# Weights and operands requested ahead of the stage that uses them, and z held feature by token

## What is computed

```python
for li in range(2):
    h = rmsnorm(x, norm_g) * (1 + scale) + shift          # same for the context hc
    if li == 0: y, yc = mixer_even(h, hc)                 # mLSTM (4 heads) and RWKV-7 (8 heads), both directions
    else:       y = column_to_raster(mixer_odd(raster_to_column(h), hc))   # HGRN (4 heads) and Hyena
    x = x + gate * y
return rmsnorm(x, final_norm_g)

# finish of the HGRN half of mixer_odd
g_y = heads_rmsnorm(from_heads(g_h), g_norm_g, HGRN_HEADS) * silu(pre['gz'])
y   = concatenate([g_y, y_y]) @ w_out
```

## Time and profile before

| | us |
|---|---|
| median of 3 runs | 2583.48 (2578.12 to 2585.52) |
| profiled execution | 2587.97 |
| its span, first to last instruction | 2585.8 |
| PE busy in the span | 2374.5 (92%) |
| DVE / ACT / POOL busy | 1434.6 / 785.2 / 229.1 |
| mean granted clock of PE | 0.96 of full speed |

### The profile page before, as it was taken

How to read it: one execution, slowest core, us unless ns; L and a number is a source line. 1 busy time by engine, 2 the same in 40 slices (tenths; PEclk the granted TensorE clock), 3 DMA queues, 4 the chain that set the end, 5 groups by cost and what they waited for, 6 DMA issues and landing times. The chain is left out here.

```text
span 2585.8 us, 52162 instructions
## 1 busy us (share of the span) xinstructions
PE 2374.5 (92%) x22964; PEld 1500.5 (58%) x22964; DVE 1434.6 (55%) x2326; ACT 785.2 (30%) x1443; POOL 229.1 (9%) x259
## 2 busy tenths in 40 slices
PE   4999999999899958998998998999898999999698
PEld 2454466666544427887884453444784676857643
DVE  5221245553367737877885454654494777778404
ACT  3111122224455623433332221101102345454301
POOL 0000000000011221111110113331100000000000
PEclk8999999999989978999999998999898999999899
DMA  6300122221065572132105422110222100000043
GB/s 259 122 11 7 33 76 66 76 72 63 30 168 163 138 180 90 61 134 101 53 28 189 143 84 66 50 56 17 82 97 81 34 26 19 25 18 10 25 172 113
DMA packets 119694, 209.23 MB, mean 81 GB/s; under 512 B 7285, under 2 KB 81141, under 8 KB 115886
## 3 DMA queue, kind: packets, MB, share of 16 engines
q1 hardware_dynamic: 105246, 152.79, 18.0%
q0 software_dynamic: 14224, 53.12, 7.2%
HBM read 155.35 MB, written 50.53 MB: 80 GB/s over the span
## 5 line engine op out<-in xcount | busy, mean ns | idle before, releaser
L786 PE MATMUL psum<-arena,m_fill_weight 128*128 128x512 f32 (+1 forms) x864 | 331.1, 528 | 6.2 <-DMA m_fill_weight<-in_l_w_in 6.2
L2707 PE MATMUL psum<-arena,g_weight 128*128 128x512 f32 (+1 forms) x512 | 224.7, 560 | 10.9 <-DMA g_weight<-in_l_w_in 10.3
L786 PEld LDWEIGHTS psum<-arena,m_fill_weight 128*128 128x128 f32 x864 | 159.5, 194 | 113.4 <-issue 98.5
L2698 PE MATMUL psum<-g_weight,arena 128*128 128x128 f32 x1152 | 157.4, 285 | 3.8 <-DMA g_weight<-in_l_w_in 3.8
L1251 PE MATMUL psum<-gp_weight,arena 128*128 128x512 f32 x320 | 147.8, 610 | 0.0
L2136 PE MATMUL psum<-fin_weight,fin_mix 128*128 128x512 f32 x320 | 143.4, 601 | 3.0 <-POOL fin_mix L2269 3.0
L2698 PEld LDWEIGHTS psum<-g_weight,arena 128*128 128x128 f32 x1152 | 141.3, 196 | 7.1 <-issue 4.4
L2707 PEld LDWEIGHTS psum<-arena,g_weight 128*128 128x128 f32 x512 | 88.6, 194 | 52.6 <-issue 35.3
L2962 DVE COPY_PREDICATED g_pairs<-g_masks,psum 128x512 f32<-128x512 uint8 x128 | 93.4, 730 | 37.2 <-PE psum L2736 36.4
L2136 PEld LDWEIGHTS psum<-fin_weight,fin_mix 128*128 128x128 f32 x320 | 59.8, 192 | 75.0 <-issue 71.5
L1251 PEld LDWEIGHTS psum<-gp_weight,arena 128*128 128x128 f32 x320 | 59.5, 194 | 72.2 <-issue 71.7
(11 more groups left out here) (443 smaller groups left out, 4309.2 us busy)
## 6 DMA issues: line engine op xcount, KB each, us to landing
arena<-scratch_operands SPq DMA_DIRECT2D x40, 512.0 KB, 3.8
scratch_operands<-arena POOLq DMA_DIRECT2D x16, 640.0 KB, 8.0
scratch_operands<-arena POOLq DMA_DIRECT2D x32, 320.0 KB, 10.7
g_weight<-in_l_w_in SPq DMA_DIRECT2D x20, 512.0 KB, 3.9
m_fill_weight<-in_l_w_in SPq DMA_DIRECT2D x18, 512.0 KB, 3.9
mod_weight<-in_l_mod_w SPq DMA_DIRECT2D x8, 1024.0 KB, 11.8
t_matrix<-in_transform SPq DMA_DIRECT2D x8, 1024.0 KB, 4.8
scratch_spill<-m_fill_shifted POOLq DMA_DIRECT2D x12, 640.0 KB, 3.2
```

Source lines behind the costliest of these rows:

```text
L786: last = nc.tensor.matmul(p.psum[:, FILL + f % BANKS, 0:width], weight[:, q % PIECES, k, :], hT[:, k, at:at + width], start=(k == 0), stop ...
L2698: last = nc.tensor.matmul(bank[:, (t - part[0]) * P:(t - part[0] + 1) * P], hT[:, kk, t * P:(t + 1) * P], w[:, kk, :], start=(kk == 0), st ...
L2707: last = nc.tensor.matmul(bank[:, 0:width], w[:, kk, :], hT[:, kk, first:first + width], start=(kk == 0), stop=(kk == KT - 1))
```

## The change

Three changes in one. (1) In the mLSTM stage `GATE_BEATS` is 20 instead of 18. (2) First layer: one buffer `shared` holds in turn the projection weights, the mLSTM fill weights, prepare's weights, the scan's values and masks, and the output weights, so that SP can load the next stage's data while a stage runs. (3) Second layer: the same with `second_shared` for Hyena's sums, HGRN's weights and gates, and the output weights; z is computed feature by token like q, and POOL multiplies it in after the turn. Semaphores of loads that cross a stage are kept for the whole program. `out_weight_of(shared)` is the first 8 x 1024 columns of the buffer. The core of the diff:

```diff
-    BANKS, PIECES, GATE_BEATS, STEP_BEATS = 2, 4, 18, 6
+    BANKS, PIECES, GATE_BEATS, STEP_BEATS = 2, M_PIECES, 20, 6
...
# stage_project, SP, after its own loads
+                if following:
+                    sp.wait_ge(products_ready, ends[len(jobs) - SLOTS])
+                    for to, of, next_loaded in following:
+                        sp.dma_start(to, of).then_inc(next_loaded, 16)
...
# stage_mlstm, SP: the first four slices are there
-                q = 0
+                q = PIECES
...
# stage_gate_and_prepare
+        v = lambda j: product[:, :] if j + 1 < R_PAIRS else kr[:, (j + 1) % 2, :]
-        opened, mixT = sb("opened", [P, 2, W]), sb("mixT", [P, 2, WT, P])
+        opened = sb("opened", [P, 2, W])
...
+        mixT = sb("mixT", [P, 3, WT, P])
...
-                sp.dma_start(kr[:, 0, :], spill[2, 0]).then_inc(kr_loaded[0], 16)
                 for i, name in enumerate(("w_up", "a_up")):
                     sp.dma_start(up[:, i, :], p.dram[name]).then_inc(sig["up_loaded"], 16)
+                sp.dma_start(kr[:, 0, :], spill[2, 0]).then_inc(kr_loaded[0], 16)
...
+                    if j + 1 < R_PAIRS:
+                        sp.wait_ge(sig["keys_ready"], 2 * j + 2)
+                    else:
+                        sp.wait_ge(sig["keys_used"], 2 * j)
+                    sp.dma_start(v(j), spill[3, j]).then_inc(sig["v_loaded" if j + 1 < R_PAIRS else "last_v_loaded"], 16)
...
+                sp.wait_ge(sig["project_ready"], UNITS)
+                sp.dma_start(scan_masks, p.dram["const_rwkv"].rearrange("p (d n) -> p d n", d=2)).then_inc(p.masks_loaded, 16)
+                sp.wait_ge(queries_stored, 48 * (ITEMS - 1))
+                sp.wait_ge(keys_stored, 48 * (ITEMS - 1))
+                window = scan_window(arena)
+                for i, c in enumerate(scan_order(0, R_CHUNKS, CTX // R_CHUNK)[0:R_EARLY]):
+                    sp.dma_start(window[:, i], operands[0, c]).then_inc(p.operands_loaded[i], 16)
+                load_values(sp, vT, spill[3], 0, R_EARLY_TOKENS, p.v_loaded)
...
# POOL, end of the block
-                pool.wait_ge(sig["bonus_stored"], 16 * R_PAIRS)
                 pool.wait_ge(queries_stored, 48 * ITEMS)
                 pool.wait_ge(keys_stored, 48 * ITEMS)
-                for i in range(2):
-                    pool.wait_ge(mix_stored[i], 16 * TILES // 2)
...
# DVE, the last gate unit ahead of the last bonus
+                    if s == END:
+                        gate(UNITS - 1)
...
# stage_rwkv_scan, SP
-                    sp.dma_start(window[:, s % SLOTS], operands[d, c]).then_inc(operands_loaded[s % SLOTS], 16)
+                    if s >= R_EARLY:
+                        sp.dma_start(window[:, s % SLOTS], operands[d, c]).then_inc(operands_loaded[s % SLOTS], 16)
+                    if s == R_EARLY + 1:
+                        load_values(sp, vT, v_dram, R_EARLY_TOKENS, TOK, v_rest_loaded)
...
# stage_transforms, SP, behind the matrices for the way back
+                for n, (_, column) in enumerate(G_AHEAD):
+                    to = shared[:, n * KT * P:(n + 1) * KT * P].rearrange("p (k n) -> p k n", k=KT)
+                    sp.dma_start(to, w_view[:, :, column:column + P]).then_inc(p.gated_weight_loaded[n], 16)
...
# stage_hgrn: z like q; SP, behind its own weight loads
-    parts = {"gate0": GROUPS, "gate1": GROUPS, "q": LAT_GROUPS, "v": v_banks, "z": ((2, 6), (6, 10)), "turn": (0, 1)}
+    parts = {"gate0": GROUPS, "gate1": GROUPS, "q": LAT_GROUPS, "v": v_banks, "z": LAT_GROUPS, "turn": (0, 1)}
+                sp.wait_ge(sig["fill_ready"], last_of["v", H - 1])
+                sp.wait_ge(sig["decay_ready"], U - 1)
+                for row in (0, 1, 2, 3, 5, 6, 7):
+                    sp.dma_start(out_weight[:, row, :], p.dram["l1_w_out"][row * P:(row + 1) * P, :]).then_inc(p.out_rows_loaded[row], 16)
+                sp.wait_ge(sig["fill_ready"], last_of["z", H - 1])
+                sp.dma_start(out_weight[:, 4, :], p.dram["l1_w_out"][4 * P:5 * P, :]).then_inc(p.out_rows_loaded[4], 16)
+                for row in OUT_AHEAD:                      # (4, 5, 6, 7, 0, 1)
+                    if row < H:
+                        sp.wait_ge(sig["stored"], 32 * (row + 1))
+                    sp.dma_start(mixT_next[:, row, CTX:TOK], mix[row, :, CTX:TOK]).then_inc(p.out_rows_loaded[row], 16)
# stage_hgrn, POOL
-                    pool.wait_ge(sig["fill_copied"], last_of["turn", head])
-                    nc.gpsimd.dma_start(mix[head, :, CTX:TOK], mixT).then_inc(sig["stored"], 16)
+                    pool.wait_ge(sig["silu_ready"], head + 1)
+                    for part in range(2):
+                        columns = slice(part * BANK, (part + 1) * BANK)
+                        pool.wait_ge(sig["fill_copied"], first_of["turn", head] + part + 1)
+                        nc.gpsimd.tensor_tensor(mixT[:, columns], mixT[:, columns], z[:, head % 2, columns], ALU.mult).then_inc(sig["gated"], 1)
+                        pool.wait_ge(sig["gated"], 2 * head + part + 1)
+                        nc.gpsimd.dma_start(mix[head, :, CTX + part * BANK:CTX + (part + 1) * BANK], mixT[:, columns]).then_inc(sig["stored"], 16)
# stage_hgrn, norm: ACT opens z in step 3 instead of step 1; DVE no longer multiplies by it
-                        then(nc.vector.tensor_tensor(out, out, z[:, h % 2, :].rearrange("p (t n) -> p t n", n=P), ALU.mult))
...
# stage_output: only rows 2 and 3 of the mix are loaded in the stage; PE takes the rows in the order 4, 5, 6, 7, 0, 1, 2, 3
-                for k in range(KT):
+                for k in OUT_ROWS[len(OUT_AHEAD):]:
                     sp.dma_start(mixT[:, k, at:TOK], mix[k, :, at:TOK]).then_inc(rows_loaded[k], 16)
-                    sp.dma_start(weight[:, k, :], p.dram[f"l{layer}_w_out"][k * P:(k + 1) * P, :]).then_inc(rows_loaded[k], 16)
```

214 lines of the change are left out of this document (123 added, 91 removed).

## The result

The changed kernel took 2554.87 us (median of 4 runs, 2551.99 to 2559.09) against 2584.5 for the kernel before beside it: ratio 0.9889, 95% interval 0.9869 to 0.9909. A second measurement of the same kernel gave 2555.01 against 2583.76, ratio 0.9895 (0.9878 to 0.9912). So it is 29 us faster; 2549 (2536 to 2564) was forecast. The profiled execution took 2559.09 (span 2556.9), 28.9 less than that of before.

The account below looks back on a forecast made before the run. PE hardly rests inside stages, so time is saved only where it stands still, its clock is low or its work shrinks. Terms 5.7 + 1.5 + 15.6 + 3.9 + 2 + 1 + 4.8 = 34.5 us: 2583.48 to 2549.0, range 2536 to 2564.

Parts of the forecast that it names:

- projections to mLSTM, beats: Start of mLSTM: prefetched weight slices save 4.2 us, less low clock 1.5; two more beats cost 0; 5.7 (4.2 to 7.2).
- mLSTM to prepare: Start of prepare: r_up halves issued ahead of the 640 KB key row; 1.5 us gained (0 to 2.5).
- prepare to scan: Prepare's end and scan's start: earlier block end, early loads and fewer waits give 15.6 us (9 to 21).
- HGRN seam: Start of HGRN: four weight slices loaded during the transforms, so PE starts 3.9 us earlier (3 to 5).
- z, and gating on GpSimd: In HGRN: wide z products gain 2 us (0 to 5.6); gating on GpSimd gains 1 (-4 to +3.7).
- HGRN to output: HGRN's tail: block ends 0.4 us later, but PE starts output at once on preloaded rows; 4.8 gained (3 to 6).
- rival B: HGRN: GpSimd's products hold DVE through the port, so gating costs 4 to 8 us instead of giving 1; 2556, chance 0.11.
- Rival A: Prepare's end: early loads hold the 320 and 640 KB stores back, prepare to scan gives 6; 2558, chance 0.16.
- the 8.8 us of scan waits: Scan's start: waits of 1.97 and 6.8 us go, with masks present and chunks 2 and 3 issued at once.
- Rival E: HGRN: GpSimd products, on every head's way to its store, hold PE's slots; slower, 2593 at 5.5 us each, chance 0.03.
- The 0.4 for GpSimd's way: HGRN's tail: GpSimd's two products and one more store's issue, less the savings, end the block 0.4 us later.
- Rival C: Shorter rests let PE keep or regain 2.4 GHz earlier: mLSTM seam 1.5 us more, scan's start 6 more; 2541, chance 0.11.

Follow-up runs that it names:

- experiment 8: Changed kernel with prepare's last stores issued by SP instead of GpSimd and their waits moved into the scan's queue: 2551.79 us, ratio 0.987.
- experiment 5: Changed kernel with two buffers instead of one for HGRN's turned rows, by head modulo 2: 2559.41 us, ratio 0.9896.

## Why the prediction was right, and where not

The mechanism was right where most of the gain lies (the seams behind the projections, ahead of HGRN and ahead of the output, the waits in the scan, z), wrong in prepare and at its end; the time is within the range and 5.9 us above the forecast. By its terms, first forecast, then measured as a difference between the two profiles, and as one of means over the table where equal code was profiled several times:

```
term                        forecast   two profiles   means
projections to mLSTM, beats    5.7         8.7          6.6
mLSTM to prepare               1.5        -3.3         -1.6
prepare to scan               15.6         9.6          9.5
HGRN seam                      3.9         3.9          3.9
z, and gating on GpSimd        2 + 1       4.5          6.1
HGRN to output                 4.8         2.0          2.3
elsewhere                      0           3.4
sum                           34.5        28.9
```

The sum is nearer than its terms, and that is partly luck: by the two profiles three terms brought 7.9 us more than forecast (mostly low clock and scatter) and three brought 13.6 less. The number alone would fit rival B (2556) or A (2558) better than the forecast's 2549; what speaks against them is in the traces. The 3.4 elsewhere are 1.3 ahead of the mLSTM seam, 1.6 between the scan and HGRN and 0.5 behind the output's first product, each no more than equal code scatters there.

**Projections to mLSTM.** The rest fell by the 4.2 forecast, and the low clock behind it, 6.8 us in both profiles of the kernel before, was gone or 3.4 (half of it was counted). The 4.5 us by which the stage itself became shorter are this low clock and the rest of it, 12.8 us within the stage before against 3.4, and in part chance: the kernel before with its loads reordered had 6.6 and took 397.73. GATE_BEATS was rightly costed at nothing, but the reason that mattered was only touched: it is not that the steps lose cover, it is that without the two beats the rest reappears at the gate's turn. Left out, it costs 8 us, all that the prefetch brings.

**mLSTM to prepare, the wrong sign.** The step "the key row then lands later, but its two ACT steps end before the LoRA matmuls do" failed. The row landed late enough for a new wait of 2.03 us, which took back most of the 2.6 won at `r_up`. What was left does not show: with the low clock at 17 us, as before, the way takes 226.1 to 226.8, and before it took 226.64. The term of 1.5 was nothing. The loss is low clock (27 us instead of 17), which came and went between profiles of equal code.

**Prepare to scan, the largest error.** PE's start at once and the 8.8 us of scan waits came true (the scan is 8.45 shorter, 7.4 on average over the changed code's profiles). What failed is "what ends the block next is the last keys' and queries' store". The wait for the stores ended at 942.13, 1.8 us later than forecast once both are counted from the bonus; then GpSimd's DRAIN held the block for 4.91 us, where the 2.8 of block end had 0.94 for it. The change takes out the waits for mix and bonus stores, but the block waits for them all the same, because GpSimd issued them. With experiment 8's stores on SP the term would be 451.07 - 16.33 - 418.54 = 16.2. Rival A (the loads hold the stores back) is real and worth 2.7 where it had 9.6, the smaller part. And the reason for the 8.8 was half wrong: not that the loads are early, but that masks stand ahead and values are split.

**z and gating.** The wide products gave 2.0 (2 forecast), as much as the scatter, so the hit is not shown. The relief of DVE gave 4.3, above its upper bound of 3.7, and less low clock came with it. Rival B's price, up to 8, measured 0.9. The row that the prediction sets beside the rule on two SBUF inputs, is not such a case: that DVE instruction is a tensor-scalar with one input. The rows above are. Rival E had no ground.

**HGRN to output.** Preloading alone, z undone, gives 18.56 - 13.38 = 5.2, as the step had it. The 0.4 for GpSimd's way was 2.8: the term left out the store of the head before, whose second half now goes out at 2418.01, while one buffer serves all heads. With two buffers (experiment 5) 13.97 - 13.38 = 0.6 is left.

**Rival C** happened in part: full clock behind the mLSTM seam, 34 us of low clock around the scan's start instead of 48, but in this profile more in prepare.

## What to carry to other kernels

Taking a wait out of a block's end did nothing while GpSimd, which ended last, still had transfers of its own in flight: look at what its DRAIN waits for, and have SP issue the last stores. Order within a queue can be worth as much as an early issue (here 4 us of a profile against 2 to 3); test it first, it costs no buffers. Before a difference of a few us between two profiles is called an effect, compare how much low clock each has in the stretch. When a stage is brought nearer to the one before, every fixed point in its schedule that waits for another engine must move by as much, or the rest comes back there.

## What the runs showed of the hardware

- A DRAIN on GpSimd at the end of a block took 3.9 to 14.5 us while its own transfers were in flight, and ended 0.9 to 1.05 us after their last packet; SP's, with its transfers in flight and the DMA engines at a share of 0.97 to 1.05, took 0.12, and GpSimd's next two, with only SP's in flight, 0.23 and 0.05.
- Eight GpSimd products of 128x512 between DVE instructions on SBUF lengthened DVE's work by 1.7 us in all, by holding three instructions with both operands in SBUF (1.75, 1.07 and 1.05 us instead of about 0.69); beside them instructions with an operand in PSUM kept their 0.28 and 0.35 us.
- Profiles of equal code differ by 2 to 9 us per stage. In the mLSTM stage, where PE never rests, the difference is how long TensorE's granted clock is 0.50: 394.44 us with none of it, 396.1 with 3.4, 397.8 with 6.8.
